# Two halves of an activation tile stored at another place in SBUF: hhi and hlo allocated after the small constants

## The reference, cut to what matters

```python
# block 1
h = h + (jax.nn.silu(a @ w_gate[i]) * (a @ w_up[i])) @ w_down[i]
# block 2, twice
gate, up = jnp.split(x @ w_in, 2, axis=-1)
return (jax.nn.silu(gate) * up) @ w_out
```

## Time and profile before

| | |
|---|---|
| median of 3 runs | 858.58 us (857.91 to 858.66) |
| the profiled execution, time | 858.66 us |
| the profiled execution, span | 856.9 us |
| TensorE busy | 832.7 us, 97% of the span |
| TensorE weight loads busy | 727.5 us, 85% |
| VectorE busy | 511.7 us, 60% |
| ScalarE busy | 430.0 us, 50% |
| mean granted TensorE clock | 0.988 of full |

### The profile page before, as it was taken

How to read it: one execution, slowest core, us unless ns; L and a number is a source line. 1 busy time by engine, 2 the same in 40 slices (tenths; PEclk the granted TensorE clock), 3 DMA queues, 4 the chain that set the end, 5 groups by cost and what they waited for, 6 DMA issues and landing times.

```text
span 856.9 us, 12471 instructions
## 1 busy us (share of the span) xinstructions
PE 832.7 (97%) x4861; PEld 727.5 (85%) x4861; DVE 511.7 (60%) x595; ACT 430.0 (50%) x562; POOL 19.7 (2%) x24
## 2 busy tenths in 40 slices
PE   6999999999999999899999999899998999999997
PEld 6977987888888888788888888799997888888886
DVE  5664444665555565665555555656777665556554
ACT  5334545644544445744444445636455644444444
POOL 0000000000000000000000000000440000000000
PEclk8999999999999999899999999999999999999999
DMA  7631222165555454265555554343245455555531
GB/s 274 261 103 50 99 99 99 57 244 191 196 196 191 181 182 180 81 241 193 196 196 187 181 181 186 102 173 144 99 148 197 173 196 197 191 180 182 187 142 49
DMA packets 20654, 141.44 MB, mean 165 GB/s; under 512 B 2432, under 2 KB 2688, under 8 KB 3984
## 3 DMA queue, kind: packets, MB, share of 16 engines
q1 hardware_dynamic: 20048, 138.92, 44.9%
q0 software_dynamic: 576, 2.10, 0.7%
HBM read 139.96 MB, written 1.05 MB: 165 GB/s over the span
## 4 chain that ended last, share of the span: by engine, by line
PE 95%; ACT 2%; DVE 1%; issue 1%; DMA 1%; DVEq 0%; SPq 0%; ACTq 0%
PE ps L1236 94%; DMA ident<-ident_in 1%; ACT squared L613 0%; ACT whi L592 0%; PE ps L1413 0%; ACT squared L602 0%; DVE x L1058 0%; DVE x L1070 0%; PE ps L1611 0%; PE ps L1392 0%; ACT stat L627 0%; PE ps L1416 0%; DVEq L260 0%; ACT stat L629 0%; DVE diag L1054 0%
## 5 line engine op out<-in xcount | busy, mean ns | idle before, releaser
L1236 PE MATMUL ps<-xa,whi 128*128 128x512 f32 (+2 forms) x1808 | 502.5, 346 | 0.0
L1236 PE MATMUL ps<-xa,wlo 128*128 128x256 f32 (+1 forms) x1408 | 394.4, 282 | 0.0
L877 DVE TENSOR_TENSOR wlo<-raw,whi 128x2048 fp32r<-128x2048 f32 x128 | 294.3, 2299 | 104.5 <-ACT whi L592 104.4
L1236 PEld LDWEIGHTS ps<-xa,whi 128*128 128x128 f32 x1808 | 314.1, 189 | 44.3 <-issue 1.0
L1236 PEld LDWEIGHTS ps<-xa,wlo 128*128 128x128 f32 x1408 | 266.0, 189 | 1.1
L592 ACT ACTIVATE whi<-raw 128x2048 fp32r<-128x2048 f32 x128 | 244.3, 1909 | 5.5 <-PE ps L1236 5.5
L1236 PE MATMUL ps<-whi,hhi 128*128 128x512 f32 x240 | 93.8, 391 | 0.0
L1236 PE MATMUL ps<-whi,hlo 128*128 128x512 f32 x240 | 93.7, 390 | 0.0
L1236 PE MATMUL ps<-wlo,hhi 128*128 128x512 f32 x240 | 93.5, 390 | 0.0
L743 ACT ACTIVATE arena<-ps 128x512 f32<-128x512 f32 x33 | 19.8, 599 | 90.8 <-PE ps L1236 90.8
L751 ACT ACTIVATE arena<-ps 128x512 f32<-128x512 f32 x33 | 19.7, 598 | 86.2 <-PE ps L1236 86.2
(11 more groups left out here) (171 smaller groups left out, 541.4 us busy)
## 6 DMA issues: line engine op xcount, KB each, us to landing
raw<-wstream SPq DMA_DIRECT2D x129, 1024.0 KB, 4.8
gain_row<-rows_in POOLq DMA_DIRECT2D x4, 512.0 KB, 4.0
const<-const_in SPq DMA_DIRECT2D x1, 1192.0 KB, 10.3
x<-x_in SPq DMA_DIRECT2D x2, 512.0 KB, 4.0
out<-x SPq DMA_DIRECT2D x4, 256.0 KB, 2.0
small<-small_in SPq DMA_DIRECT2D x1, 152.0 KB, 5.8
ident<-ident_in SPq DMA_DIRECT2D x1, 64.0 KB, 4.5
arena<-meta_in SPq DMA_DIRECT2D x1, 64.0 KB, 4.4
```

The costliest lines, as they stand in the source:

```text
L877: nc.vector.tensor_tensor(wlo[slot][:], raw[slot][:], whi[slot][:].bitcast(F32), ALU.subtract).then_inc(lo_ready, 1)
L1236: return nc.tensor.matmul(o, lhsT, rhs, start=start, stop=stop, skip_group_check=True)
```

## The change

`hhi` and `hlo` are allocated behind `stat` instead of behind `ya`. Nothing else is changed.

```diff
         xa = sb("xa", [P, KT, 2 * TOK], F32R)
         ya = sb("ya", [P, KT, 2 * SEQ], F32R)
-        hhi = sb("hhi", [P, 2, 256], F32R)
-        hlo = sb("hlo", [P, 2, 256], F32R)
         x = sb("x", [P, TT, D])
         gain_row = sb("gain_row", [P, D])
...
         eps = sb("eps", [P, 1])
         stat = sb("stat", [P, 40])
+        hhi = sb("hhi", [P, 2, 256], F32R)
+        hlo = sb("hlo", [P, 2, 256], F32R)
         arena = sb("arena", [P, ARENA])
```

## The result

The changed kernel is slower: 864.72 us median of 4 runs (862.91 to 865.23) against 858.62 us, ratio 1.0067 with a 95% interval of 1.005 to 1.0085, so 6.1 us. I had forecast no change, 858.6 us, with 860.7 as the upper end. Its profiled execution took 864.48 us, with a span of 862.7 us, 5.8 us more than the earlier trace rows.

A forecast was written before the change was run, and what follows sets the result against it. TensorE, busy 832.7 of 856.9 us, was taken to bound the kernel. All terms (moved tensors, writes, loads, matmul distance) were 0, so the time stayed at 858.6 us, range 857.1 to 860.7 us.

The forecast's parts named there:

- What bounds the kernel: Whole kernel: TensorE bounds it, busy 832.7 of 856.9 us, with no hole in a feed-forward layer.
- The tensors x to stat: Tensors moved by 4096 bytes, keeping their place relative to powers of two up to 4096; taken as 0.
- Writing hhi and hlo: 30 ScalarE copies and 30 VectorE subtractions: -13 to +1 ns each, off the path; taken as 0.
- Loading them: 720 weight loads from hhi and hlo in down units: -2 to +4 ns each, hidden; taken as 0, uncovered 2.9 us.
- The distance between matmuls: Start-to-start time of down-unit matmuls, 228 ns: no change from the stationary operand's place; 0, bounds -0.7 and +1.4 us.
- the row nearest in kind: Small gate weights, loaded at 32 modulo 64 under moving xa: 0.35 against 0.36 us per three matmuls, cited for no change.
- The turns: Stretches between stages where TensorE waits for the norm: lower clock may fall differently, but gives the same time.
- clash: Down units: loaded hhi and moved whi pieces no longer start alike modulo 512, saving up to 10.8 us; chance 0.05.
- neighbour theory: Down units: hhi and hlo beside arena, which ScalarE and VectorE use, slow matmuls by 1.7 to 5.0 us; chance 0.08.
- slower eight: First eight matmuls of a down unit, 230 ns each against 227 for the other sixteen, coinciding with a ScalarE copy.
- the long load: Down units: loads at an odd place hold the path over 228 ns; at 250 ns, 15.8 us more; chance 0.02.

The follow-up runs named there:

- new_128: Changed kernel with padding bringing hhi and hlo, still between stat and arena, back to start 128 modulo 512; 858.03 us, ratio 0.9995 to the kernel before.
- old_480: Kernel before with padding around hhi and hlo, at their old place, giving start 480 modulo 512 as in the changed kernel; 865.13 us, ratio 1.0069.
- the second sweep: TensorE alone, not the kernel: loaded pieces over 135 KB above the moved one, finer starts, also 256 moved columns (117.3 to 120.1 ns) and 32-column loads.
- the sweep: TensorE alone, not the kernel: groups of 24 512-column matmuls, loaded or moved piece shifted in 32-byte steps; 226.7 to 234.3 ns per matmul.
- m128b: Group of 24 matmuls in the TensorE-alone sweep that shifts the moved piece, here with loaded and moved piece both at 128 modulo 512; 226.8 ns settled.
- xa_2304: Kernel before with rows of xa 2304 instead of 2176 bytes apart, so all start at the same place modulo 256; 866.72 us, ratio 1.01.

## Why the prediction was wrong

**What bounds the kernel** was right: what was added between the matmuls of a down unit came through whole, 145 ns a unit, 30 times.

**The tensors x to stat** at 0: right, by `new_128` and `old_480`. **Writing hhi and hlo** at 0: right, 632 and 692 ns as before. **Loading them**: right in its own term, 188 ns before and after. But I took the load's duration for all that a load can do. It is read beside the moved operand, and the price is in the matmul: 397 ns instead of 389 at the median, with the same load.

**The distance between matmuls** is the step that failed. I set it at 0, with bounds of -0.7 and +1.4 us, by the small gate weights of the earlier trace rows, "the row nearest in kind". The true term is 720 x 6.04 ns = 4.35 us. I chose that row for a start of 32 modulo 64, and that is no measure of anything. It has 256 moved columns, where the second sweep finds a range of 2.8 ns over all distances and no gain at distance 0, while for 512 columns the range is 7.6 ns and distance 0 is the best. It runs under an `xa` whose rows alternate between two starts modulo 256, and so does the row I compared it with, so neither has what the down unit had, the same start for all loads and all moved pieces, and neither could show what its loss costs. And the two rows don't quite agree: three matmuls take 350 ns each time with the small weights, and 361 and 352 in turn with `whi` and `wlo`, 2 ns more per matmul. I rounded this to 0.01 us and read it as no dependence. The slots and layers that agreed to a nanosecond were no evidence either: all their starts are 8192 bytes apart, a multiple of 256, which can't show it.

**The turns** failed as well, as a smaller term. I gave the clock there the same time, on three runs 0.75 us apart. At the median the loss is 6.1 us and the down units explain 4.4; the other 1.7 us are, as far as the profiles show, time at the turns, where the two profiles of the changed kernel have 38.6 and 37.4 us for the same stretch. With the down units' term alone the time would be 863 us, already above my range.

The rivals: the **clash** had the right mechanism, the starts of the loaded and the moved piece, with the sign turned round. I asked what a coincidence of starts costs today, and not what it might be saving. That the kernel before had one of the 8 best of 64 starts follows from tensors whose sizes are multiples of 256 bytes; I hadn't asked. A neighbour theory had the size (5.0 us) and the place in the program, but `old_480` and `new_128` refute its cause. The coincidence in time of the slower eight with ScalarE's copy was chance: the sweep has such matmuls at the head of a group too (230, 236, 228, 233, 230 and then 227 in the group `m128b`, at distance 0), with ScalarE idle.

One mark that I had named did its work: a down unit of over 5.53 us, spread over all 24 matmuls. I had given that to the long load; it is the distance.

The Trainium skill, "TensorE: Matmul & The Clock Gate", section "Step-by-step: what each phase is for", says of TensorE's two read ports: "Loading the next tile's weights doesn't steal SBUF read bandwidth from the running matmul." The runs here don't bear this out as it stands: with the same load of 188 ns the matmuls beside it last 389 or 397 ns at the median by where the two pieces start, and the interval is 226.7 to 237.4. The measurement decides. The Trainium skill's "SBUF — State Buffer", section "Specifications (TRN2)", by which I had counted lines of 16 bytes, does not reach this either: pieces at 124 and at 132 touch 33 lines of 16 bytes each, and have 226.7 and 232.4 ns.

## What to carry to other kernels

Where TensorE has no gap, compare the start-to-start distance of matmuls by kind before and after a change of the layout: a tensor allocated elsewhere can cost 3% of each fp32r matmul that has its own load, without any wait or longer load in the profile. A stream of equal 512-column matmuls was at its best here when the loaded and the moved piece started at the same place modulo 256 (and at 7 other starts of 64), and a tensor put ahead of them with an uneven size is enough to lose that; a down unit's own figure in the timeline shows it at once. Don't carry the rule over to alternating shapes without measuring it in the kernel: there all rows at distance 0 had 353 ns a pair against 348, though TensorE alone had 347 for the same starts. And take a row as evidence only if it has the same shape as the one in question: 256-column matmuls said nothing about 512-column ones.

## What the runs showed of the hardware

- The interval of 512-column fp32r matmuls with a load of 128 columns each was 226.7 to 237.4 ns at 2.4 GHz (213.3 for the columns), by the distance of the two starts modulo 256, in steps as small as 4 bytes; the loads had a median of 187 or 188 ns in all of them. With 256 columns it was 117.3 to 120.1 ns.
- At distance 0 and at 96 it was the same with ScalarE, VectorE and the queues at work and idle, and at distance 0 the same with the pieces 135 KB apart.
- The intervals of a group are no noise but a repeating pattern (seven in a row at 231 to 238 ns in the changed kernel, then the same seven again), and they depend on what ran before: the down units of `xa_2304` need ten matmuls until they settle at 227 ns, those of the kernel before seven.
- A load of 32 columns, 108 ns long, made the interval longer (231.6 and 239.7 ns) than one of 128 columns at the same two distances (226.7 and 233.4).
- At the turns the granted clock differed between executions of one program (0.87 and 1.00 in the same 12 us of the changed kernel), and with it the length of a turn by over 1 us.
